# Output product of the token mixers in split one-pass products

## Chip, cores and metric

One core of a Trainium2 chip runs the whole program. The metric is the device time in microseconds (us) of one execution. Three executions of the kernel before took 1275.85, 1275.85 and 1276.56 us, median 1275.85.

Engines: PE is TensorE, ACT is ScalarE, DVE is VectorE, POOL is GpSimd, SP issues most DMAs. PEld is the weight load of a product, which overlaps the product before it.

## What is computed

A decoder trunk of two layers on 256 tokens of width 1024. In each layer three token mixers (attention with a window, a selected and a compressed branch; a convolution; retention) read one input projection, and their concatenated output goes through `w_out`. A dense SwiGLU follows on layer 0, an expert SwiGLU (2 of 8) on layer 1.

```python
def token_mixer(h, w_in, ..., w_out):
    proj = h @ w_in
...
    o_a = nsa_mixer(q, k_c, v_c, k_s, v_s, k_w, v_w, gl, cmp_pe, cmp_w1, cmp_w2)
    o_b = conformer_conv(conv_in, conv_w, conv_b, conv_ln_g, conv_ln_b, conv_pw)
    o_c = retention(rq, rk, rv, rg, ret_gn)
    return jnp.concatenate([o_a, o_b, o_c], axis=-1) @ w_out

for l in range(DEPTH):
    h = rmsnorm(x, ln_attn[l])
    x = x + token_mixer(h, ...)
    h = rmsnorm(x, ln_ffn[l])
    x = x + (swiglu(h, ...) if l % 2 == 0 else moe_ffn(h, ...))
```

## The kernel before, in words

The five engines have instruction streams of their own, written by hand, and each executes its stream strictly in order. In a mixer all engines walk one list of stages, `MIXER[l]`: for each entry an engine issues what it has to do for that stage, or nothing. So one table (`HEAD`, `AHEAD`, `BESIDE`, `TAIL`) sets the order on PE, ACT and DVE at once, and moving an entry moves it on all of them. PSUM banks are handed out round robin along that list (`GROUP`); an engine says that a bank is full (`is_full`) or free (`is_free`), and others wait with `full` and `freed`.

The middle of a mixer is twelve attention units k = 0 to 11. In unit k, PE transposes the probabilities of unit k (`probT`, L664), runs the scores of unit k + 2 (`score`), the entries of `BESIDE[k]`, and then probability by value (`pv`). ACT copies the transposed probabilities from PSUM (L1308), exponentiates the scores of unit k + 2 (L1298), then does its share of `BESIDE[k]`. DVE takes the maximum of the scores (L1705, L1707), which the exponentials wait for, then does its share of `BESIDE[k]`, then scales the result of `pv` (L1712, L1716, L1719). `BESIDE` places the convolution, the retention, the compressed branch and the output product between the units.

The output product has four banks: `out` k is token tile i = k // 2 and column half h = k % 2. Its first stage `out` multiplies rows 4 to 7 of `catT` (convolution in 4, 5, written by ACT in `conv_pw`; retention in 6, 7, by ACT in `retcat`) by `w_out`, four full fp32 products of 512 columns. Its second stage, `out_rest`, adds rows 0 to 3 (attention, in `attn_sum`) in four more. An fp32 product is recorded as two matmuls. Then DVE adds the bank to `x` (L1833), PE transposes `x` (`xT`), and in layer 0 DVE and ACT split the result into a high and a low half (L1841, L1380, L1845).

Elsewhere the kernel already uses split products: a float32 operand becomes a high part in fp32r (a copy on ACT) and a low part (raw minus high, on DVE), and `three` adds high x high, high x low, low x high, each in one pass. `pre` makes the first feed-forward weights ready: per half two copies of 1024 words a partition on ACT (L1390) and one subtraction of 2048 on DVE (L1869).

```python
def three(o, ah, al, bh, bl, first, final):
    mm(o, ah, bh, first, False)
    mm(o, ah, bl, False, False)
    return mm(o, al, bh, False, final)
...
elif stage == "out":
    ...
        for c in range(KD // 2, KD):
            mm(o, catT[:, c, i * P:(i + 1) * P], w[:, c, :], c == KD // 2, False)
```

Of the kernel before, what the change touches and what calls it, by code (L numbers as in the profile page):

```python
# [7 lines left out]
F32 = mybir.dt.float32  # L8
# [7 lines left out]
P = 128  # L16
# [60 lines left out]
def conv(a, b):  # L77
# [76 lines left out]
VW, RET, CONV, QK, W1K, W1VN, WO = range(7)  # L154
LAST_READ = (None, ("rqk", 1, 0), ("kcv", 0, 0), ("ks", 0, 0), ("cmpkv", 0, 0), ("cmpkv", 0, 0),
# [105 lines left out]
def hybrid_trunk_kernel(nc, x_in, consts_in, params_in, mix_in, ffn_in, moe_in, router_in, final_in, out):  # L261
    with ExitStack() as ctx:
# [57 lines left out]
        ro = mix("ro", [P, NT, RET_HEADS, HD])  # L320
        gates = mix("gates", [P, NT, HEADS, 3])
# [22 lines left out]
        cacc = mix("cacc", [P, 2, NC, T])  # L344
# [54 lines left out]
        whM = [nc.alloc_sbuf_tensor_at(f"whM{h}", [P, KD, FC], F32R, offset=home_at[h]) for h in range(4)]  # L399
        beforeb = sb("beforeb", [P, P], BF16)  # L400
# [77 lines left out]
        s_rk = sem("s_rk")  # L478
        s_conv_in = [sem(f"s_conv_in{h}") for h in range(2)]
# [179 lines left out]
        def _(pe):  # L659
# [24 lines left out]
            def width_major(o, l, n, half):  # L684
# [5 lines left out]
                return last  # L690

# [49 lines left out]
            def mixer(l):  # L741
                for stage, k in MIXER[l]:
# [219 lines left out]
                    elif stage == "out":  # L962
# [1317 lines left out]
```

## Time and profile before

| | |
|---|---|
| median of 3 executions | 1275.85 us |
| the profiled execution | 1274.48 us |
| its span, first to last instruction | 1272.5 us |
| busy PE / PEld / DVE / ACT | 98% / 80% / 78% / 67% |
| TensorE clock granted, mean | 0.997 |
| chain that ended last | PE 92%, DVE 4%, ACT 2%, DMA 1%, issue 1% |
| layer 0 mixer / dense / layer 1 mixer / experts | to 158 / to about 350 / to 496 / to 1264 us |

The profiled execution lies 1.4 us under the median, and its span 2.0 us under its own time. A busy PE is not PE at its peak, since the ends of matmuls are modelled; what counts is the distance of starts.

### The profile page before, as it was taken

Reading aid. Unit: us, or ns where it says so; the run is one execution under the profiler, and the core shown is the slowest. Engines: PE = TensorE matmul, PEld = TensorE weight load, DVE = VectorE, ACT = ScalarE, POOL = GpSimd, SP = SyncE. Lnnn points to the kernel's source line nnn. Section 1 sums busy time; section 2 is a strip of 40 time slices with the busy share of each in tenths; the row PEclk is TensorE's granted clock in tenths of the full one; section 3 lists DMA queues with packets and bytes.
Section 4 is the critical chain, followed back from the end, with each engine's and each line's share of the span. In section 5 each row is a group of like instructions: output and inputs, shape, how many; then the busy total and the mean of one; then the engine's idle time right before and its main releaser. Section 6 shows DMA issues by size and latency. Waiting matters only on the chain.

```text
span 1272.5 us, 16272 instructions
## 1 busy us (share of the span) xinstructions
PE 1253.3 (98%) x6317; PEld 1015.6 (80%) x6317; DVE 996.7 (78%) x1110; ACT 857.3 (67%) x1225; POOL 31.4 (2%) x21
## 2 busy tenths in 40 slices
PE   9999999999999999999999999999999999999997
PEld 8797588888779866788888888888888888888885
DVE  4786465454569646998999989889889889889997
ACT  5435364444451544978878888878878878878885
POOL 0000000000000000010000000000000000000300
PEclk9999999999999999999999999999999999999998
DMA  9433194442521336899999999999999999999981
GB/s 366 169 143 133 67 387 174 175 190 103 198 100 71 143 132 271 335 404 373 391 371 371 389 380 375 388 369 377 396 369 379 389 374 357 396 373 353 416 368 39
DMA packets 38625, 367.62 MB, mean 289 GB/s; under 512 B 4112, under 2 KB 7312, under 8 KB 11152
## 3 DMA queue, kind: packets, MB, share of 16 engines
q1 hardware_dynamic: 35808, 356.56, 71.2%
q0 software_dynamic: 1440, 5.24, 1.1%
q10 hardware_dynamic: 1296, 4.72, 0.9%
q8 instruction: 53, 0.87, 0.3%
q14 instruction: 28, 0.23, 0.1%
HBM read 360.73 MB, written 5.77 MB: 288 GB/s over the span
## 4 chain that ended last, share of the span: by engine, by line
PE 92%; DVE 4%; ACT 2%; DMA 1%; issue 1%; SPq 0%; DVEq 0%; ACTq 0%
PE ps L661 88%; PE ps L664 3%; DMA ring<-mix_in 1%; ACT arena L1298 1%; DVE blocks L1687 1%; DVE wlU L1869 1%; DVE arena L1705 0%; DVE wlD L1876 0%; ACT arena L1308 0%; ACT L1290 0%; ACT L1345 0%; DVE arena L1778 0%; DVE xn L2112 0%; DVE hTl L1991 0%; DVE x L1833 0%
## 5 line engine op out<-in xcount | busy, mean ns | idle before, releaser
L1869 DVE TENSOR_TENSOR wlU<-ring,whU 128x2048 fp32r<-128x2048 f32 x196 | 448.9, 2290 | 57.7 <-ACT whU L1390 53.1
L1390 ACT ACTIVATE whU<-ring 128x1024 fp32r<-128x1024 f32 x396 | 417.6, 1060 | 60.8 <-PE ps L661 53.2
L661 PE MATMUL ps<-whU,hTh 128*128 128x512 f32 x880 | 352.7, 401 | 0.8 <-DVE wlU L1869 0.8
L661 PE MATMUL ps<-whU,hTl 128*128 128x512 f32 x880 | 345.0, 392 | 0.0
L661 PE MATMUL ps<-wlU,hTh 128*128 128x512 f32 x880 | 342.9, 390 | 0.0
L1876 DVE TENSOR_TENSOR wlD<-ring,whD 128x2048 fp32r<-128x2048 f32 x97 | 222.2, 2290 | 39.2 <-ACT whD L1402 39.0
L1402 ACT ACTIVATE whD<-ring 128x1024 fp32r<-128x1024 f32 x194 | 205.2, 1066 | 59.0 <-PE ps L661 52.8
L661 PEld LDWEIGHTS ps<-whU,hTl 128*128 128x128 f32 x880 | 165.1, 188 | 36.0
L661 PEld LDWEIGHTS ps<-wlU,hTh 128*128 128x128 f32 x880 | 166.1, 189 | 32.4
L661 PEld LDWEIGHTS ps<-whU,hTh 128*128 128x128 f32 x880 | 165.3, 188 | 32.7 <-DVE wlU L1869 1.0
L661 PE MATMUL ps<-whD,gTh 128*128 128x512 f32 x428 | 168.6, 394 | 0.5 <-DVE gTl L1894 0.5
L661 PE MATMUL ps<-whD,gTl 128*128 128x512 f32 x428 | 167.3, 391 | 0.0
L661 PE MATMUL ps<-wlD,gTh 128*128 128x512 f32 x428 | 166.6, 389 | 0.0
L661 PEld LDWEIGHTS ps<-whD,gTh 128*128 128x128 f32 x428 | 80.4, 188 | 19.7 <-DVE wlD L1876 3.6
L661 PEld LDWEIGHTS ps<-whD,gTl 128*128 128x128 f32 x428 | 80.3, 188 | 16.9
L661 PEld LDWEIGHTS ps<-wlD,gTh 128*128 128x128 f32 x428 | 80.7, 189 | 16.4
L1416 ACT ACTIVATE gTh<-ps 128x256 fp32r<-128x256 f32 x107 | 40.3, 386 | 54.6 <-PE ps L664 54.6
L661 PEld LDWEIGHTS ps<-arena 128*128 128x128 f32 (+1 forms) x472 | 56.6, 190 | 14.5 <-issue 12.7
L661 PE MATMUL ps<-arena 128*128 128x64 f32 (+6 forms) x472 | 65.2, 297 | 2.3 <-ACT arena L1308 2.3
L1894 DVE TENSOR_TENSOR gTl<-ps,gTh 128x256 fp32r<-128x256 f32 x107 | 44.3, 422 | 27.5 <-ACT gTh L1416 27.5
L664 PE MATMUL ps<-cst,arena 128*128 128x128 f32 x376 | 63.3, 273 | 1.2 <-DVE arena L1815 1.1
L664 PEld LDWEIGHTS ps<-cst,arena 128*128 128x128 f32 x376 | 48.2, 143 | 17.2 <-issue 3.6
(232 smaller groups left out, 1224.2 us busy)
## 6 DMA issues: line engine op xcount, KB each, us to landing
ring<-moe_in SPq DMA_DIRECT2D x88, 2048.0 KB, 8.5
ring<-moe_in SPq DMA_DIRECT2D x88, 1024.0 KB, 8.6
ring<-ffn_in SPq DMA_DIRECT2D x11, 2048.0 KB, 7.5
ring<-mix_in SPq DMA_DIRECT2D x5, 3072.0 KB, 11.0
ring<-ffn_in SPq DMA_DIRECT2D x11, 1024.0 KB, 7.2
ring<-mix_in SPq DMA_DIRECT2D x4, 2048.0 KB, 10.3
ring<-mix_in SPq DMA_DIRECT2D x2, 2176.0 KB, 8.3
ring<-mix_in SPq DMA_DIRECT2D x2, 2112.0 KB, 8.1
```

What stands on the lines that cost most here:

```text
L661: return nc.tensor.matmul(o, lhsT, rhs, start=first, stop=last, skip_group_check=True)
L664: return nc.tensor.transpose(o, a, ident)
L1298: last = A(prob[:, k % 3, c * keys:(c + 1) * keys], bank(l, stage, k)[:, c * keys:(c + 1) * keys], ACT.Exp, bias=nmax[:, k, c:c + 1], scal ...
L1390: A(whU[:, p, :], ring[:, f.slot(J), p * PIECE:(p + 1) * PIECE], ACT.Copy).then_inc(s_hi, 1)
L1402: A(wh_down(f, J, c), ring[:, f.slot(J), (UP + c) * PIECE:(UP + c + 1) * PIECE], ACT.Copy)\
L1416: A(g_high(f, J, i), ps[:, up_bank(f, J, i), 0:FC].rearrange("p (c t) -> p c t", c=DOWN), ACT.Copy)\
L1687: last = V.tensor_tensor(blocks[lo:lo + HD, v, hi, :, g, 0:NBLK], src[g * HD:(g + 1) * HD, v, :, hi:hi + NBLK, r], spread(pe_[lo:lo + HD, ...
L1869: V.tensor_tensor(wlU[:, w, :], raw, whU[:, w, :].bitcast(F32), ALU.subtract).then_inc(s_lo, 1)
L1876: V.tensor_tensor(wl_down(f, J), raw, high.bitcast(F32), ALU.subtract).then_inc(s_lo, 1)
L1894: V.tensor_tensor(g_low(f, J, i), ps[:, up_bank(f, J, i), 0:FC].rearrange("p (c t) -> p c t", c=DOWN), g_high(f, J, i).bitcast(F32), ALU.s ...
```

## The change

`out` and `out_rest` are made of split one-pass products. For that, each layer gets:

- a stage `wo` k, k = 0 to 7: a quarter of one column half of `w_out` (two rows c of 512, 1024 words a partition). ACT copies it to `woh` (high), DVE writes raw minus high back over the raw words in the ring. `BESIDE[5]` to `BESIDE[11]` get one each, `TAIL` the last. PE waits for `s_wol` before each pair of rows.
- the concatenation in two parts: ACT writes `cath` (where `catT` was), DVE now also reads the bank and writes `catl`, and it is DVE that frees the bank. This holds for `conv_pw`, `retcat` and `attn_sum`.
- another order: `retcat` moves from unit 8 to unit 9, `out` 0 from unit 8 to 9, `out` 1 from 9 to 11, `out` 3 from 11 to `TAIL`; both `pre` stages come later in `TAIL`.

```diff
-AHEAD = {6: [("convB", 0), ("hidT", 0), ("hidT", 1), ("rsilu", 0), ("rroot", 0)], 8: [("retcat", 0)]}
+AHEAD = {6: [("convB", 0), ("hidT", 0), ("hidT", 1), ("rsilu", 0), ("rroot", 0)], 9: [("retcat", 0)]}
...
-          3: [("reto", 0), ("hid", 0), ("cnorm", 0)], 4: [("croot", 0), ("hid", 1), ("retnorm", 0)], 5: [("cnorm", 1)],
-          6: [("retnorm", 1)], 7: [("cmpkv", 0), ("conv_pw", 0)],
-          8: [("cscore", 0), ("out", 0)], 9: [("out", 1)],
-          10: [("cprobT", 0), ("out", 2), ("cpv", 0), ("cpv", 1)],
-          11: [("out", 3), ("asum", 0), ("asum", 1), ("osum", 0), ("attn_sum", 0)]}
-
-TAIL = [("osum", 1), ("pre", 0), ("out_rest", 0), ("attn_sum", 1), ("pre", 1), ("out_rest", 1), ("out_rest", 2), ("xT", 0),
-        ("xT", 1), ("out_rest", 3), ("xT", 2), ("xT", 3)]
+          3: [("reto", 0), ("hid", 0), ("cnorm", 0)], 4: [("croot", 0), ("hid", 1), ("retnorm", 0)],
+          5: [("cnorm", 1), ("wo", 0)], 6: [("retnorm", 1), ("wo", 1)], 7: [("cmpkv", 0), ("conv_pw", 0), ("wo", 2)],
+          8: [("cscore", 0), ("wo", 3)], 9: [("out", 0), ("wo", 4)],
+          10: [("cprobT", 0), ("out", 2), ("wo", 5), ("cpv", 0), ("cpv", 1)],
+          11: [("out", 1), ("wo", 6), ("asum", 0), ("asum", 1), ("osum", 0), ("attn_sum", 0)]}
+
+TAIL = [("osum", 1), ("wo", 7), ("out", 3), ("out_rest", 0), ("attn_sum", 1), ("pre", 0), ("out_rest", 1), ("out_rest", 2),
+        ("pre", 1), ("xT", 0), ("xT", 1), ("out_rest", 3), ("xT", 2), ("xT", 3)]
...
+WO_ROWS = ((0, 4), (0, 6), (0, 0), (0, 2), (1, 4), (1, 6), (1, 0), (1, 2))
...
+            def out_row(l, o, i, h, c, first, final):
+
+                if c % 2 == 0:
+                    pe.wait_ge(s_wol, len(WO_ROWS) * l + WO_ROWS.index((h, c)) + 1)
+                t = slice(i * P, (i + 1) * P)
+                low = ringl[:, mix_load(l, WO + h) % SLOTS, 512 * c:512 * (c + 1)]
+                return three(o, cath[:, c, t], catl[c // 2][:, c % 2, t], woh[l][2 * h + (c < 4)][:, c % 4, :], low, first, final)
...
+                    elif stage == "wo":
+                        h, c = WO_ROWS[k]
+                        n = mix_load(l, WO + h)
+                        act.wait_ge(slot_full[n % SLOTS], filled(n))
...
+                        A(wo_high(l, k), wo_rows(ring, l, k), ACT.Copy).then_inc(s_woh, 1)
...
+                    elif stage == "wo":
+                        dve.wait_ge(s_woh, len(WO_ROWS) * l + k + 1)
+                        V.tensor_tensor(wo_rows(ringl, l, k), wo_rows(ring, l, k), wo_high(l, k).bitcast(F32), ALU.subtract)\
+                            .then_inc(s_wol, 1)
+                    elif stage in ("conv_pw", "retcat"):
+                        m = 4 if stage == "conv_pw" else 6
+                        dve.wait_ge(s_cath, CATS * l + (m == 6) + 1)
+                        is_free(V.tensor_tensor(catl[m // 2][:], bank(l, stage).rearrange("p (q t) -> p q t", q=2),
+                                                cath[:, m:m + 2, :].bitcast(F32), ALU.subtract), l, stage)
```

DVE in layer 0 from the end of the compressed branch's softmax in unit 8 to the maximum of unit 11's scores. Before:

```order
L1761 TENSOR_REDUCE arena<-arena 128x16 [waits s_cexp]
L1762 RECIPROCAL arena<-arena 128x16 [waits v_done]
L1763 TENSOR_TENSOR arena<-arena 128x16 [waits v_done]
L1765 TENSOR_TENSOR arena<-arena,cst 128x128 x2
L1768 TENSOR_TENSOR arena<-arena 128x256 [waits v_done]
L1712 RECIPROCAL arena<-arena 128x2 [waits s_exp]
L1716 TENSOR_TENSOR arena<-arena 128x2 [waits v_done]
L1719 TENSOR_TENSOR arena<-ps,arena 128x128 [waits bank_full0,v_done]
L1705 TENSOR_REDUCE arena<-ps 128x2 [waits bank_full2]
L1707 TENSOR_SCALAR arena<-arena 128x2 [waits v_done]
```

With the change (line numbers are those of the changed kernel):

```order
L1798 TENSOR_REDUCE arena<-arena 128x16 [waits s_cexp]
L1799 RECIPROCAL arena<-arena 128x16 [waits v_done]
L1800 TENSOR_TENSOR arena<-arena 128x16 [waits v_done]
L1802 TENSOR_TENSOR arena<-arena,cst 128x128 x2
L1805 TENSOR_TENSOR arena<-arena 128x256 [waits v_done]
L1856 TENSOR_TENSOR ringl<-ring,woh_75 128x1024 [waits s_woh]
L1749 RECIPROCAL arena<-arena 128x2 [waits s_exp]
L1753 TENSOR_TENSOR arena<-arena 128x2 [waits v_done]
L1756 TENSOR_TENSOR arena<-ps,arena 128x128 [waits bank_full7,v_done]
L1861 TENSOR_TENSOR catl_86<-ps,cath 128x512 [waits s_cath]
L1742 TENSOR_REDUCE arena<-ps 128x2 [waits bank_full2]
L1744 TENSOR_SCALAR arena<-arena 128x2 [waits v_done]
```

The piece `wo` 3 and the low half of `retcat`, whose end frees `out` 0, now stand behind the softmax and ahead of the next maximum.

ACT in layer 0 from the exponentials of unit 8 to those of unit 10's scores. Before:

```order
L1298 ACTIVATE arena<-ps,arena 128x256 [waits bank_full5,s_amax]
L1298 ACTIVATE arena<-ps,arena 128x256
L1308 ACTIVATE arena<-ps 128x512 [waits s_exp,bank_full6,bank_full4]
L1298 ACTIVATE arena<-ps,arena 128x128 [waits bank_full0,s_amax]
L1298 ACTIVATE arena<-ps,arena 128x128 x3
L1355 ACTIVATE arena<-ps 128x512 [waits s_exp,bank_full1]
L1308 ACTIVATE arena<-ps 128x512 [waits bank_full3,bank_full7]
L1355 ACTIVATE arena<-ps 128x512 [waits bank_full4]
L1298 ACTIVATE arena<-ps,arena 128x256 [waits bank_full6,s_amax]
```

With the change:

```order
L1325 ACTIVATE arena<-ps,arena 128x256 [waits bank_full5,s_amax]
L1325 ACTIVATE arena<-ps,arena 128x256
L1392 ACTIVATE woh_74<-ring 128x1024 [waits s_exp,slot_full0]
L1335 ACTIVATE arena<-ps 128x512 [waits bank_full6,bank_full4]
L1325 ACTIVATE arena<-ps,arena 128x128 [waits bank_full0,s_amax]
L1325 ACTIVATE arena<-ps,arena 128x128 x3
L1382 ACTIVATE cath<-ps 128x512 [waits s_exp,bank_full1]
L1392 ACTIVATE woh_75<-ring 128x1024 [waits slot_full0]
L1335 ACTIVATE arena<-ps 128x512 [waits bank_full3,bank_full7]
L1325 ACTIVATE arena<-ps,arena 128x256 [waits bank_full6,s_amax]
```

Each copy of probabilities (L1308, now L1335) stands behind a copy of weights, and `retcat`'s copy has left.

DVE in layer 0 at the end of the mixer, from the first sum into `x`. Before:

```order
L1833 TENSOR_TENSOR x<-ps,x 128x512 [waits bank_full4]
L1869 TENSOR_TENSOR wlU<-ring,whU 128x2048 [waits s_hi]
L1833 TENSOR_TENSOR x<-ps,x 128x512 [waits bank_full5]
L1833 TENSOR_TENSOR x<-ps,x 128x512 [waits bank_full6]
L1841 TENSOR_TENSOR hT<-ps,par 128x4x128 [waits bank_full2]
```

With the change:

```order
L1886 TENSOR_TENSOR x<-ps,x 128x512 [waits bank_full4]
L1867 TENSOR_TENSOR catl_83<-ps,cath 128x2x128 [waits s_cath]
L1867 TENSOR_TENSOR catl_84<-ps,cath 128x2x128
L1922 TENSOR_TENSOR wlU<-ring,whU 128x2048 [waits s_hi]
L1886 TENSOR_TENSOR x<-ps,x 128x512 [waits bank_full5]
L1886 TENSOR_TENSOR x<-ps,x 128x512 [waits bank_full6]
L1922 TENSOR_TENSOR wlU<-ring,whU 128x2048 [waits s_hi]
L1894 TENSOR_TENSOR hT<-ps,par 128x4x128 [waits bank_full2]
```

The second subtraction of `pre` now stands between the third sum into `x` and the first use of the transposed `x`.

## Rows read from the trace of the kernel before

**Rows 1.** Page, part 4, the chain that ended last: shares of the span
```profile
PE 92%; DVE 4%; ACT 2%; DMA 1%; issue 1%; SPq 0%; DVEq 0%; ACTq 0%
```

**Rows 2.** Chain in order of time, layer 0: start us, us, what
```profile
107.42 0.60 ACT arena L1308
...
114.10 0.61 ACT arena L1308
...
114.84 1.08 PE ps L661 x8
...
136.92 3.44 PE ps L661 x8
...
145.61 6.88 PE ps L661 x16
```

**Rows 3.** Timeline of PE in the dense stage: start, duration; eleven starts apart
```profile
200.03 0.39 PE L661 MATMUL ps<-whD,gTl 128*128 128x512 f32 x1
...
202.53 0.39 PE L661 MATMUL ps<-wlD,gTh 128*128 128x512 f32 x1
```

**Rows 4.** Groups by line, whole program: busy us, mean ns | idle before
```profile
L1390 ACT ACTIVATE whU<-ring 128x1024 fp32r<-128x1024 f32 x396 | 417.6, 1060 | 60.8 <-PE ps L661 53.2 <-ACT ystage L1494 3.2
L1862 DVE TENSOR_TENSOR wlU<-ring,whU 128x1024 fp32r<-128x1024 f32 x4 | 4.8, 1224 | 4.5 <-ACT whU L1390 4.5
L1894 DVE TENSOR_TENSOR gTl<-ps,gTh 128x256 fp32r<-128x256 f32 x107 | 44.3, 422 | 27.5 <-ACT gTh L1416 27.5
L1841 DVE TENSOR_TENSOR hT<-ps,par 128x512 f32<-128x512 f32 x4 | 2.7, 682 | 0.0
L1196 ACT ACTIVATE xn<-x 128x512 f32<-128x512 f32 x20 | 12.5, 624 | 17.2 <-DVE x L1833 8.2 <-DVE x L1914 4.0 <-DMA x<-x_in 3.4
```

**Rows 5.** Timeline of ACT and DVE in layer 0, units 6 to 8
```profile
115.85 0.17 DVE L1707 TENSOR_SCALAR arena<-arena 128x4 f32<-128x4 f32 x1
116.05 0.37 ACT L1298 ACTIVATE arena<-ps,arena 128x128 f32<-128x128 f32 x1 [1.35 <-DVE arena L1707]
117.68 0.60 ACT L1355 ACTIVATE arena<-ps 128x512 f32<-128x512 f32 x1
118.54 0.17 DVE L1707 TENSOR_SCALAR arena<-arena 128x2 f32<-128x2 f32 x1
119.70 0.62 DVE L1750 SCALAR_TENSOR_TENSOR arena<-ps,cst 128x64 f32<-128x64 f32 x4 [0.99 <-PE ps L661]
123.06 0.42 DVE L1768 TENSOR_TENSOR arena<-arena 128x256 f32<-128x256 f32 x1
```

**Rows 6.** Chain in order of time, end of layer 0's mixer and layer 1's: start us, us, what
```profile
152.52 0.69 DVE x L1833
...
157.19 0.61 DVE x L1833
...
491.66 0.70 DVE x L1833
```

**Rows 7.** Busy time by stretch: PE, PEld, DVE, ACT, POOL, clock, DMA
```profile
119.60:131.00 11.40, 11.40 (x51) 7.17 (x50) 5.43 (x22) 3.23 (x12) 0.00 (x0) 1.00 0.41 172
131.00:144.00 13.00, 13.00 (x49) 7.18 (x48) 4.14 (x9) 4.52 (x7) 0.00 (x0) 1.00 0.00 1
```

**Rows 8.** The same at the program's end, after PE's last product
```profile
1264.00:1265.00 1.00, 0.00 (x0) 0.00 (x0) 1.00 (x4) 0.79 (x3) 0.00 (x0) 1.00 0.00 0
1265.00:1266.00 1.00, 0.00 (x0) 0.00 (x0) 0.96 (x2) 0.89 (x3) 0.00 (x0) 0.86 0.06 16
1266.00:1267.00 1.00, 0.00 (x0) 0.00 (x0) 1.00 (x3) 0.83 (x4) 0.00 (x0) 0.50 0.00 0
```

**Rows 9.** Timeline of PE: last product; filler products at the start and in layer 1
```profile
1263.51 0.39 PE L661 MATMUL ps<-yel,gTh 128*128 128x512 f32 x1
...
1.12 5.91 PE L661 MATMUL ps<-warm 128*128 128x256 bf16 x30 [1.12 <-POOL warm L2146]
...
496.45 1.69 PE L661 MATMUL ps<-warm 128*128 128x256 bf16 x14
```

More of the change, by code:

```diff
@@ L399, in hybrid_trunk_kernel @@
         whM = [nc.alloc_sbuf_tensor_at(f"whM{h}", [P, KD, FC], F32R, offset=home_at[h]) for h in range(4)]
+        wo_at = (xn_at, hT_at, ring_at + 4 * 4096, arena_at + 4 * mix_at["rp0"])
+        woh = [[nc.alloc_sbuf_tensor_at(f"woh{l}{q}", [P, 4, 512], F32R,
+                                        offset=wo_at[q] + 4 * SLOT * (mix_load(l, WO + 1) % SLOTS) * (q == 2))
+                for q in range(4)] for l in range(DEPTH)]
+        cath = nc.alloc_sbuf_tensor_at("cath", [P, KD, T], F32R, offset=arena_at + 4 * mix_at["catT"])
+        catl = [nc.alloc_sbuf_tensor_at(f"catl{q}", [P, 2, T], F32R,
+                                        offset=arena_at + 4 * (mix_at["cln"], mix_at["csq"], mix_at["cacc"], mix_at["cacc"] + 512)[q])
+                for q in range(4)]
         beforeb = sb("beforeb", [P, P], BF16)
@@ L478, in hybrid_trunk_kernel @@
         s_rk = sem("s_rk")
+        s_woh = sem("s_woh")
+        s_wol = sem("s_wol")
+        s_cath = sem("s_cath")
         s_conv_in = [sem(f"s_conv_in{h}") for h in range(2)]
@@ L540, in piece_of, with wo_rows, wo_high @@
             return w[:, :, col:col + FC]
+        def wo_rows(buf, l, q):
+            h, c = WO_ROWS[q]
+            return buf[:, mix_load(l, WO + h) % SLOTS, 512 * c:512 * (c + 2)].rearrange("p (c n) -> p c n", c=2)
+        def wo_high(l, q):
+            h, c = WO_ROWS[q]
+            return woh[l][2 * h + (c < 4)][:, c % 4:c % 4 + 2, :]
         def half_of(i, h):
@@ L1349, in mixer @@
                         full(act, l, stage, k)
-                        is_free(A(catT[:, 0:4, k * P:(k + 1) * P],
-                                  bank(l, stage, k).rearrange("p (q t) -> p q t", q=4), ACT.Copy), l, stage, k)
+                        A(cath[:, 0:4, k * P:(k + 1) * P], bank(l, stage, k).rearrange("p (q t) -> p q t", q=4), ACT.Copy)\
+                            .then_inc(s_cath, 1)
                     elif stage in ("conv_pw", "retcat"):
@@ L1354, in mixer @@
                         m = 4 if stage == "conv_pw" else 6
-                        is_free(A(catT[:, m:m + 2, :], bank(l, stage).rearrange("p (q t) -> p q t", q=2), ACT.Copy),
-                                l, stage)
+                        A(cath[:, m:m + 2, :], bank(l, stage).rearrange("p (q t) -> p q t", q=2), ACT.Copy)\
+                            .then_inc(s_cath, 1)
+                    elif stage == "wo":
+                        h, c = WO_ROWS[k]
+                        n = mix_load(l, WO + h)
+                        act.wait_ge(slot_full[n % SLOTS], filled(n))
+                        if k == 0:
+                            full(act, l, "kcv")
+                        elif k == 6:
+                            full(act, l, "retcat")
+                        A(wo_high(l, k), wo_rows(ring, l, k), ACT.Copy).then_inc(s_woh, 1)
                     elif stage == "pre":
@@ L1374, in mixer @@
                             act.wait_ge(s_root, NT * 3 + i + 1)
+                            full(act, l, "out", 2)
                             A(xh[:, i, :], x[:, i, :], ACT.Copy, scale=stat[:, 3, i:i + 1]).then_inc(s_xh, 1)
@@ L1816, in mixer @@
                             .then_inc(s_cln, 1)
+                    elif stage == "wo":
[7 more added lines that the diff above has]
+                                                cath[:, m:m + 2, :].bitcast(F32), ALU.subtract), l, stage)
+                    elif stage == "attn_sum":
+                        dve.wait_ge(s_cath, CATS * l + 2 + k + 1)
+                        t = slice(k * P, (k + 1) * P)
+                        for q in range(2):
+                            last = V.tensor_tensor(catl[q][:, :, t], bank(l, stage, k).rearrange("p (q t) -> p q t", q=4)
+                                                   [:, 2 * q:2 * q + 2, :], cath[:, 2 * q:2 * q + 2, t].bitcast(F32), ALU.subtract)
+                        is_free(last, l, stage, k)
                     elif stage == "asum":
```

15 lines of the change are left out of this document (6 added, 9 removed).

## Prediction

> **What bounds the kernel now.** I read the page's chain first [rows 1]: PE carries 92% of the span, so whatever leaves PE's path can shorten it, and whatever makes PE wait lengthens it. Then the chain in order of time through the middle of layer 0's mixer [rows 2]. It runs over ACT from the exponentials of unit 7 to the copy that starts at 114.10, and from 114.84 it stays on PE until the third sum into x at 152.52 [rows 6]. So the mixer has two halves: up to unit 7 the handshakes of ACT and DVE set the pace, from there PE does. In the second half PE is busy without a gap, while DVE is idle for half of the time and ACT for more than that [rows 7]. Layer 1 repeats layer 0 some 334.8 us later (the same rows, the same gaps; only the tail differs).
>
> **What it removes.** Four fp32 products of 512 columns take 3.44 us [rows 2], as the 6.88 for two stages confirms. In the dense stage eleven starts of one-pass products span 2.50 us [rows 3], 0.227 each, so twelve take 2.73. I take that for the new products, whose operands have the same shape. A stage saves 0.71 us, and eight stages in two layers save 16 x 0.71 = **11.4 us** of PE work.
>
> **What it adds.** Per layer on ACT eight copies of 1024 words at 1.06, on DVE eight subtractions of the same size at 1.22, two of 512 words at about 0.68 and four of 256 words at 0.42 [rows 4]. That is 8.5 us on ACT and 12.8 us on DVE. By busy time there is room for it. But these engines run in order, and each piece is put between two links of the loop that feeds PE: maximum (DVE), exponentials (ACT), piece (ACT), piece (DVE), scaling of pv (DVE), next maximum (DVE). I walk that loop through layer 0 in the times of the trace, with its durations and start distances. No DMA is added, and the second half of `w_out` is requested when the compressed branch's product is full, long before `wo` 4; SP's next loads wait for the end of `out_rest` as before, and need not be early.
>
> - Units 5 and 6: `wo` 0 and `wo` 1 stand on ACT ahead of the copies that start at 107.42 and 114.10 [rows 2], where ACT is the chain. Each costs 0.95 (the next starts while one drains). pv 7 on PE starts at 116.7 instead of 114.84: **+1.9**.
> - Unit 6 on DVE: `wo` 1's subtraction waits for ACT (116.1) and ends at 117.4; with the scaling behind it (0.74) and the maximum the exponentials of unit 9 start at 118.95 instead of 116.05 [rows 5].
> - Unit 7: ACT needs 1.6 for those exponentials, then `conv_pw`'s copy at 120.6 (117.68 before), then `wo` 2 to 122.1, then the copy of probabilities 8 to 122.6. PE, at cscore 2.0 late, is idle some 1.6 us until pv 8 at 122.75; before, `out` 0 filled that place. DVE takes `conv_pw`'s low half to 121.9, `wo` 2 to 123.4, the scaling to 124.0, and has the maximum of unit 10 ready at 124.8. Before, that was 118.7 [rows 5].
> - Unit 8: the softmax of the compressed branch starts at 124.75 instead of 119.70 and ends after 3.8 us (119.70 to 123.48 [rows 5]) at 128.5. Then `wo` 3 to 129.6, the scaling of pv 8 to 130.2, and only then the low half of `retcat`, to 130.8. That one frees `out` 0.
> - PE: pv 8, the transposes and the scores of unit 11 are done by 125.4. Then it waits for `retcat` until 131.0: **5.6 us idle**, the largest term.
> - From there PE has 12.7 us of work up to the end of `out` 1 (three stages at 2.73 and what the trace has between them), to 143.7. The attention sum needs both `asum` and `osum`, which stand behind `wo` 6 on DVE, which waits for ACT's copy behind the last copy of probabilities. They end at 146.2: **2.5 us idle**.
> - The rest of PE's work is 12.7 us to the end of `out_rest` 2 at 159.0. DVE ends the third sum at 160.1, but then `pre` 1's subtraction (2.2) stands ahead of the first use of the transposes. The chain of the tail, 4.6 us between the two sums in layer 0 [rows 6], becomes 6.8. The fourth sum ends at 166.9 instead of 157.8: layer 0 is **9.1 us** longer.
> - Layer 1: the same up to `out_rest`. There ACT's share of `pre` 1 stands behind two squares at 0.62 [rows 4] and a root, about 2 us together, and DVE waits for it. The fourth sum ends 11.2 us later than it does now (at 491.66 [rows 6]): **+11.2**.
>
> The sum is 9.1 + 11.2 = 20.3 us, after the 11.4 that PE saves. Nothing behind the mixers gets less work: dense and expert stages are PE without a gap and take the shift as it is.
>
> **The clock.** The trace of before has no PE idle of 5 us inside the program. Its nearest row is the end: the last product starts at 1263.51 [rows 9], the granted clock is still full until 1265, 0.86 in the next microsecond and 0.50 from 1266 [rows 8]. So it falls within some 2 us of idling, and a gap of 5.6 us before `out` 0 should see it fall. What that costs: at the kernel's start 30 filler products took 5.91 us, 0.197 each, in layer 1 fourteen took 1.69, 0.12 each [rows 9]. For 30 that is a loss of 2.3 to 2.7 us, the second with the last one's latency left out. The ends are 0 (the clock holds) and 2.7; I take 2.7 per layer since the end of the program is the nearest row: **+5.4 us**. The Trainium skill ("TensorE: Matmul & The Clock Gate", "Why this matters for your kernels") says that an idle gap between bursts of matmuls brings the half clock back. By that rule 2.7 per layer stands, without it the time would be that of the second rival. The end of this trace agrees with it (0.50 after the last product).
>
> Sum against the profiled execution: 1274.48 + 20.3 + 5.4 = 1300.2. That execution lies 1.4 us under the median, so the forecast is **1301.6 us** for the median, 2.0% more.
>
> **Rivals.**
> - *The clock falls at the tails too.* PE is idle for 3 to 5 us there, broken only by transposes. Two more times 2.7: 1307.
> - *The clock holds.* For it speaks that it was never below 1.00 in the mixers, though PE does little there. 1275.85 + 20.3 = 1296.
> - *The waits are half as long.* My walk adds handshakes one after another; if ACT and DVE absorb half of the net loss, +10: 1286.
> - *PE's saving wins, faster.* The place is the stretch from 114.84 on. Where DVE and ACT are idle for half of the time [rows 7], all pieces could fit into those gaps, and then 11.4 us come off: 1264.5. It decides if `retcat`'s low half is ready when PE reaches `out` 0, that is at 125.4 and not at 130.8. Against it: DVE's gaps are waits for PE, and its stream is in order. The Trainium skill ("Perfetto Trace Analysis", "Identifying the Most-Contended Engine") would have the engine with the highest occupancy optimized first, which is PE here, and by that rule the time would be this one; the 92% of the chain [rows 1] agree, the ACT rows at 107.42 and 114.10 [rows 2] do not.
> - *The change doesn't do what it says.* If weight loads did not hide behind the new products, a product might cost what an fp32 record costs now, 0.43 (3.44 by eight [rows 2]), a stage 5.2 instead of 2.73. Half of the sixteen stages would show in full after the waits: 8 x 2.5 = +20, 1322. The dense stage has the same form without it [rows 3].
>
> **How the numbers follow.** Chances: forecast 0.37, clock holds 0.27, waits half as long 0.14, clock falls at the tails too 0.10, faster 0.06, no one-pass gain 0.04, and 0.02 for gains and losses that cancel. The range has to hold 8 in 10: from 1284, just under the halved waits, to 1309, just over the fourfold fall; only the last three cases lie outside. A measurement can tell about 0.2% (2.6 us) from no change. Slower: 0.37 + 0.27 + 0.14 + 0.10 + 0.04 = 0.92; same 0.02; faster 0.06.
>
> **What would show it.** In the changed profile: twelve products from first to last in 2.5 to 2.8 us; the copies of probabilities 6 and 7 each about 1 and 2 us later against the trace of before; PE idle for 5 to 6 us ahead of the first product of `out` 0, released by the DVE subtraction of `retcat`; 2 to 3 us idle ahead of `attn_sum` 0, released by `osum`; the second subtraction of `pre` between the third sum and hT. The start of dense at about 167.5 instead of 158.3. Under full clock those gaps alone give +20; a clock row under 1.00 right after the first gap decides between forecast and second rival. If the gap ahead of `out` 0 is under 2 us, the walk over units 6 to 8 is wrong and the time is nearer 1280 or below. If a product there takes 0.4 and not 0.23, the price of the products is.

## The result, and the profile after

| | before | after |
|---|---|---|
| median of 4 executions each | 1275.85 us | 1306.53 us |
| ratio | 1 | 1.0244 (1.0231 to 1.0256) |
| span of the profiled execution | 1272.5 us | 1305.2 us |
| TensorE clock granted, mean | 0.997 | 0.98 |
| dense stage starts | 158.3 us | 171.65 us |
| first product of the experts | 504.81 us | 537.01 us |

The kernel became 30.7 us slower; 1301.6 was forecast. The trace of after starts 0.77 us earlier than that of before (the exponentials of unit 7 at 105.45 against 106.22), so 0.77 is added below wherever its times are compared with forecast ones. Layer 0's mixer took 172.4 - 158.3 = 14.1 us more, layer 1's 32.2 - 13.35 = 18.9 more. These are 33.0 and not 30.7, since the profiled execution of before lies 1.4 us under its median and that of after 0.7 over.

The chain's shares by engine on the page, to be read against [rows 1], where PE had 92%:

```profile
PE 90%; DVE 5%; ACT 3%; issue 2%; DVEq 0%; POOL 0%; ACTq 0%; POOLq 0%
```

PE lost two points to DVE, ACT and "issue", though it had less to compute. What it waited for is shown by the view of waits (who waited, for whom, us in total, times, the longest). Of before:

```profile
PE ps L661 <- ACT arena L1308: 2.3, 6, 0.5
```

Of after:

```profile
PE ps L684 <- ACT arena L1335: 6.3, 7, 2.0
PE ps L684 <- issue: 6.3, 2, 3.7
PE ps L687 <- DVE arena L1878: 4.7, 2, 2.3
PE ps L687 <- DVE x L1886: 4.1, 3, 3.4
PE ps L687 <- DVE hTr L1894: 3.3, 1, 3.3
```

The first is the copy of probabilities, behind a piece. The second is the gap ahead of `out` 0, which the profile puts down to nobody: it ends with `retcat`'s low half. The third is `osum`, the last two are sums and turned rows of the tail, behind the late `pre`. In the timeline of layer 0 (start, duration, engine, what; in brackets the idle time before it and who ended it) each is one line:

```profile
107.60 0.58 ACT L1335 ACTIVATE arena<-ps 128x512 f32<-128x512 f32 x1
115.17 0.58 ACT L1335 ACTIVATE arena<-ps 128x512 f32<-128x512 f32 x1
115.90 1.54 PE L684 MATMUL ps<-arena 128*128 128x64 f32 x8 [1.99 <-ACT arena L1335]
118.11 0.37 ACT L1325 ACTIVATE arena<-ps,arena 128x128 f32<-128x128 f32 x1 [2.36 <-DVE arena L1744]
123.75 0.17 DVE L1744 TENSOR_SCALAR arena<-arena 128x2 f32<-128x2 f32 x1
129.27 0.68 DVE L1861 TENSOR_TENSOR catl<-ps,cath 128x512 fp32r<-128x512 f32 x1
130.05 0.77 PE L684 MATMUL ps<-woh,cath 128*128 128x512 f32 x1 [3.73 <-issue]
130.62 0.63 PE L684 MATMUL ps<-ringl,cath 128*128 128x512 f32 x1
131.05 0.63 PE L684 MATMUL ps<-woh,catl 128*128 128x512 f32 x1
...
135.86 0.48 PE L684 MATMUL ps<-woh,cath 128*128 128x512 f32 x1
...
138.51 0.40 PE L684 MATMUL ps<-woh,catl 128*128 128x512 f32 x1
138.74 2.71 PE L684 MATMUL ps<-arena 128*128 128x512 f32 x12
...
147.00 1.04 PE L687 MATMUL ps<-cst,arena 128*128 128x128 f32 x4 [2.33 <-DVE arena L1878]
147.83 1.81 PE L684 MATMUL ps<-arena 128*128 128x64 f32 x8
148.71 0.76 DVE L1867 TENSOR_TENSOR catl<-ps,cath 128x256 fp32r<-128x256 f32 x2 [1.85 <-ACT cath L1377]
149.40 0.77 PE L684 MATMUL ps<-woh,cath 128*128 128x512 f32 x1
...
154.31 0.40 PE L684 MATMUL ps<-woh,cath 128*128 128x512 f32 x1
...
170.93 1.07 PE L687 MATMUL ps<-cst,x 128*128 128x128 f32 x4 [3.42 <-DVE x L1886]
```

The twelve products of `out` 2 start between 135.86 and 138.51, 2.65 us for eleven distances, and the next stage starts at 138.74: 2.88 us for the stage, close to the 2.73 of the forecast. But the products of `out` 0 behind the gap start 0.43 apart instead of 0.24. Busy time by stretch, with the granted clock as the third number from the end, says why:

```profile
116.00:118.00 2.00, 2.00 (x12) 2.00 (x13) 1.90 (x7) 0.00 (x0) 0.00 (x0) 0.58 0.94 393
...
124.00:126.00 2.00, 2.00 (x7) 1.35 (x5) 1.45 (x7) 1.59 (x6) 0.00 (x0) 0.50 0.08 33
126.00:128.00 2.00, 0.32 (x1) 0.00 (x0) 1.90 (x7) 1.72 (x3) 0.00 (x0) 0.86 0.00 0
128.00:130.00 2.00, 0.00 (x0) 0.00 (x0) 1.93 (x6) 0.00 (x0) 0.00 (x0) 1.00 0.00 0
130.00:132.00 2.00, 1.95 (x5) 1.59 (x6) 0.72 (x2) 1.09 (x5) 0.00 (x0) 0.50 0.00 0
...
150.00:152.00 2.00, 2.00 (x6) 1.61 (x5) 1.87 (x3) 0.00 (x0) 0.00 (x0) 0.50 0.00 0
...
172.00:174.00 2.00, 2.00 (x6) 1.52 (x6) 1.29 (x2) 0.64 (x3) 0.00 (x0) 0.50 1.08 459
```

In layer 0 the clock is at its lower level (0.50, 1.2 GHz) not once but behind each of the waits: after the 2 us ahead of `pv` 7, again in unit 8, after the gap ahead of `out` 0, after the 2.3 us ahead of `attn_sum` 0, and after the 3.4 us ahead of the last transposes. In layer 1 it is 0.50 from 520 to 532 us, and the 32 router products there took 6.83 us; 3.64 before. But not every wait brings it down. Layer 1 has the same wait ahead of `pv` 7, and there the clock stays full behind it; it falls at 471 us, with two more waits (0.52 us ahead of 469.05, 1.03 ahead of 472.04):

```profile
466.04 1.08 PE L684 MATMUL ps<-arena 128*128 128x64 f32 x8 [1.98 <-ACT arena L1335]
...
466.00:468.00 2.00, 1.96 (x16) 1.93 (x17) 1.93 (x5) 0.00 (x0) 0.00 (x0) 1.00 1.03 442
468.00:470.00 2.00, 1.49 (x21) 1.11 (x19) 0.87 (x4) 1.63 (x9) 0.00 (x0) 1.00 0.98 418
```

So the clock falls at five places in layer 0 and at four in layer 1.

### The profile page after: what moved, and what is told of

It reads as the page before. It is cut to its first block, busy times and chain, and to the rows that moved or that the text cites. A ratio compares the mean times of both kernels' runs of the same rounds, so it can differ in the third digit from the quotient of the medians.

```text
span 1305.2 us, 16458 instructions
## 1 busy us (share of the span) xinstructions
PE 1265.8 (97%) x6381; PEld 1044.1 (80%) x6381; DVE 1021.0 (78%) x1138; ACT 872.5 (67%) x1241; POOL 28.8 (2%) x21
## 4 chain that ended last, share of the span: by engine, by line
PE 90%; DVE 5%; ACT 3%; issue 2%; DVEq 0%; POOL 0%; ACTq 0%; POOLq 0%
PE ps L684 86%; PE ps L687 4%; DVE wlU L1922 1%; ACT arena L1325 1%; DVE blocks L1724 1%; DVE arena L1742 0%; ACT whU L1427 0%; DVE wlD L1929 0%; ACT woh L1392 0%; ACT arena L1335 0%; DVE x L1886 0%; DVE arena L1874 0%; ACT xn L1223 0%; ACT L1317 0%; ACT L1372 0%
## 5 line engine op out<-in xcount | busy, mean ns | idle before, releaser
L684 PE MATMUL ps<-arena 128*128 128x64 f32 (+6 forms) x472 | 70.3, 311 | 6.8 <-ACT arena L1335 6.3
L684 PEld LDWEIGHTS ps<-arena 128*128 128x128 f32 (+1 forms) x472 | 60.4, 201 | 17.6 <-issue 14.6
```

The source lines that it names most:

```text
L684: return nc.tensor.matmul(o, lhsT, rhs, start=first, stop=last, skip_group_check=True)
```

## The experiments

Two claims were to be tested: that the waits come from pieces set in order into the loop over ACT and DVE, and that the clock takes the rest. Ratios are to runs of before on the same chip, whose median was 1274.9 to 1275.5 us.

### The order alone

Tables of the change without the `wo` stages, on the kernel before.

```diff
-AHEAD = {6: [...], 8: [("retcat", 0)]}
+AHEAD = {6: [...], 9: [("retcat", 0)]}
...
-          8: [("cscore", 0), ("out", 0)], 9: [("out", 1)],
+          8: [("cscore", 0)], 9: [("out", 0)],
...
-TAIL = [("osum", 1), ("pre", 0), ("out_rest", 0), ("attn_sum", 1), ("pre", 1), ("out_rest", 1), ("out_rest", 2), ("xT", 0),
-        ("xT", 1), ("out_rest", 3), ("xT", 2), ("xT", 3)]
+TAIL = [("osum", 1), ("out", 3), ("out_rest", 0), ("attn_sum", 1), ("pre", 0), ("out_rest", 1), ("out_rest", 2),
+        ("pre", 1), ("xT", 0), ("xT", 1), ("out_rest", 3), ("xT", 2), ("xT", 3)]
```

> Left out of the change: the split products, the eight pieces per layer and the low halves of the concatenation; only the new order of retcat, out and pre is kept, with fp32 products. Theory (the pieces and low halves, put between the links of the loop over ACT and DVE, make most of the waits): PE has the same work as before, out 0 no longer fills unit 8 (some 1 to 2 us per layer), and the second subtraction of pre stands in the tail (2.2 us in layer 0, some 4 in layer 1): 1276 + 9 = 1285 us (1280 to 1291), no clock row under 0.95 in the mixers but perhaps at the tails. Rival (the order itself is the cause: out no longer covers the units): the waits of the change are nearly all there, and without the 11.4 us that PE saves the time is 1305 or more.

Measured: 1284.8 us, ratio 1.0081 (1.0064 to 1.0097), +9.6 us. The rival falls. That the time is the expected one is in part luck: unit 8, which was to cost 1 to 2 us per layer, costs 0.4 in layer 0 (from the exponentials of unit 7 to the third sum 46.7 us against 46.3), and the clock, which the sum had at nothing, is 0.50 for some 14 us in layer 1's tail. The waits are those of the tail:

```profile
PE ps L664 <- DVE x L1833: 3.5, 2, 2.9
...
PE ps L664 <- DVE hTr L1841: 2.0, 1, 2.0
```

### The pieces alone

```diff
-          5: [("cnorm", 1)], 6: [("retnorm", 1)], 7: [("cmpkv", 0), ("conv_pw", 0)],
-          8: [("cscore", 0), ("out", 0)], 9: [("out", 1)],
+          5: [("cnorm", 1), ("wo", 0)], 6: [("retnorm", 1), ("wo", 1)], 7: [("cmpkv", 0), ("conv_pw", 0), ("wo", 2)],
+          8: [("cscore", 0), ("out", 0), ("wo", 3)], 9: [("out", 1), ("wo", 4)],
...
+                    elif stage == "wo":
...
+                        V.tensor_tensor(wo_high(l, k), wo_rows(ring, l, k), wo_high(l, k).bitcast(F32), ALU.subtract)\
+                            .then_inc(s_wol, 1)
```

> Kernel before with its order and its fp32 products, plus the eight pieces per layer (ACT's copy, DVE's subtraction) at the units where the change has them; their results are used by nothing. Theory: units 5 and 6 are ACT's path, so pv 7 comes 1.9 us later per layer; behind it out 0 and out 1 cover the pieces; in the tail the last piece costs up to 1 us: 1276 + 2 x 2.5 = 1281 us (1278 to 1288), clock full. Rival (ACT and DVE absorb the pieces): 1276 to 1277. Rival (the loop walks later by every piece, also under out 0 and out 1): 1276 + 2 x 8 = 1292 or more.

Measured: 1290.9 us, ratio 1.0127 (1.0110 to 1.0144), +15.7. My own number missed; the time lies by that of the last rival. Timeline of PE in layer 0 (this trace starts 0.46 us earlier than that of before):

```profile
116.21 1.08 PE L678 MATMUL ps<-arena 128*128 128x64 f32 x8 [1.98 <-ACT arena L1325]
...
120.07 1.96 PE L678 MATMUL ps<-arena 64*128 64x16 f32 x32 [0.92 <-ACTq L1320]
122.65 2.05 PE L678 MATMUL ps<-ring,arena 128*128 128x512 f32 x2 [0.62 <-ACT arena L1372]
...
146.63 0.63 PE L681 MATMUL ps<-cst,arena 128*128 128x128 f32 x4 [1.66 <-DVE arena L1855]
```

`pv` 7 is 1.8 us late as expected, but that isn't the end: the exponentials of unit 9 stand behind it, and `out` 0 starts at 122.65 where it started at 119.60, 3.5 us late with the offset. Up to there the clock is full, behind the wait of 1.98 us too; it is 0.61 and 0.54 in the rows from 122 to 126, and the piece `wo` 6 ahead of `asum` costs 1.7 more. `out` 0 hides nothing that was lost before it. In the prediction I had followed the loop through unit 7; in this expectation I stopped at `pv` 7.

### Holding the clock

```diff
+                        if k in (7, 8):
+                            keep_busy(o, 16 if k == 7 else 8)
...
+                            keep_busy(o, 42)
...
+                        if k == 0:
+                            keep_busy(o, 20)
...
+                        if k >= 2:
+                            keep_busy(ps[:, OUT_BANK[0], :], ((4, 28), (40, 6))[l][k - 2])
```

> The changed kernel plus bf16 filler products on PE in the gaps ahead of pv 7, pv 8, out 0, attn_sum 0 and the transposes of the third and fourth sums, sized by the trace to end before the wait does. Theory (the granted clock falls at four or five places of each mixer, not at one, and that costs about 10 us): 1306.5 - 10 = 1296.5 us (1294 to 1300), clock rows near 1.00 through both mixers. Rival (the low clock only falls where PE waits anyway): 1304 to 1308.

Measured: 1296.3 us, ratio 1.0168 (1.0151 to 1.0185), mean clock 0.995. That is 10.2 us less than the change (9.7 by the two ratios), for products that compute nothing. The rival falls. What is left, 21.1 us over before, is within 1 us of the 20.3 to which my walk of waits had come, and the layers agree one by one: 8.9 and 12.5 us more in this trace, 9.1 and 11.2 in the walk. One fall is left, in layer 1's tail (0.50 from 516 to 523 us), so 10.2 is the least that the clock took.

### `pre` back at its early places, alone and with the fillers

```diff
-TAIL = [..., ("out_rest", 0), ("attn_sum", 1), ("pre", 0), ("out_rest", 1), ("out_rest", 2), ("pre", 1), ("xT", 0), ...
+TAIL = [..., ("pre", 0), ("out_rest", 0), ("attn_sum", 1), ("pre", 1), ("out_rest", 1), ("out_rest", 2), ("xT", 0), ...
```

> The changed kernel with both pre stages back at their places in the order of before. Theory (the second subtraction of pre, 2.2 us, stands on the path of the tail; in layer 1 ACT's share of about 2 us too): 2.2 + 4.2 less, plus a clock that may hold at the tail: 1306.5 - 6.4 = 1300 us (1297 to 1303). Rival (the earlier pre pushes the low halves of the attention sum and the first sum into x later by as much): 1305 to 1309.

Measured: 1294.4 us, ratio 1.0151 (1.0134 to 1.0168): 12.1 us less than the change, more than either theory gave.

> The changed kernel with both edits that were tried alone: fillers ahead of pv 7, pv 8, out 0 and attn_sum 0 (not in the tail), and both pre stages back at their early places. Alone they gave 10.2 us (fillers, the tail's among them) and 12.1 us (pre). Theory (pre's own wait is 6.4 us and the rest of its 12.1 is the clock that no longer falls at the tail, so the two share the tail's part of the clock): 1306.5 - 10.2 - 6.4 = 1290 us (1288 to 1292). Rival (separate causes that add up in full): 1284. Rival (both are the clock alone): 1294 to 1296.

Measured: 1289.0 us, ratio 1.0110 (1.0095 to 1.0125), where the theory said 1290. So the two edits overlap. With the clock held, the early `pre` gives 1296.3 - 1289.0 = 7.3 us: that is its wait (my walk had 2.2 + about 4; the two traces show 2.2 in layer 0 and 4.4 in layer 1). Without it, 12.1: the other 4.8 are clock that the late `pre` took in the tails. In the traces the clock is low in the tails for some 17 us with the change and some 3 us with the early `pre`, and in units 6 to 11 for about as long in both. And with the early `pre` the fillers give 1294.4 - 1289.0 = 5.4: the clock behind the waits ahead of `pv` 7, `out` 0 and `attn_sum` 0. Each of these differences is uncertain by some 2 us, since the ratios' intervals reach 0.0015 to 0.0017 to either side.

### Which half of a piece, and POOL as the place for them

In the kernel with the subtractions on POOL, ACT keeps the copies:

```diff
-                    elif stage == "wo":
-                        dve.wait_ge(s_woh, len(WO_ROWS) * l + k + 1)
-                        V.tensor_tensor(wo_rows(ringl, l, k), ...
+                for k in range(len(WO_ROWS)):
+                    pool.wait_ge(s_woh, len(WO_ROWS) * l + k + 1)
+                    G.tensor_tensor(wo_rows(ringl, l, k), ...
```

> The changed kernel, but only the eight subtractions per layer go to POOL; ACT keeps the eight copies. It tells which half of a piece costs. Theory (both halves stand in the loop; ACT's cost about 2 us per layer up to unit 7 and again at its copies of probabilities later, DVE's the rest, above all ahead of the maximum of unit 10 and the low half of retcat): 1306.5 less about 12 = 1294 us (1288 to 1300). Rival (ACT's copies alone make it): 1303 to 1308. Rival (DVE's subtractions alone): near what the kernel with all pieces on POOL takes.

Measured: 1298.7 us, ratio 1.0188 (1.0171 to 1.0205), 7.8 less than the change. The counterpart has the copies on POOL (`G.tensor_copy`) and the subtractions on DVE:

> The counterpart of the kernel with the subtractions on POOL: the changed kernel with the eight copies per layer on POOL (early, as soon as the half of w_out is there) and the eight subtractions left on DVE. Theory (ACT's copies are half of the handshake, and a copy on POOL holds DVE up for at most its own 1.04 us, where the subtraction of 2.4 us held it for as long): DVE does not wait for ACT's copy any more, units 5 and 6 lose nothing: 1306.5 - 9 = 1297 us (1292 to 1301). Rival (DVE's subtractions alone bind units 7 and 8): 1303 to 1308. Rival (POOL's copies stretch DVE's short operations on the path of units 4 and 5): 1305 or more, with DVE operations of two operands in SBUF over 1 us long.

Measured: 1297.5 us, ratio 1.0172 (1.0155 to 1.0189), 9.0 less. Neither half makes the loss by itself; each is a link of the loop. How much each takes stays open, since POOL holds DVE up in both (below). Then both halves on POOL, in the order of the change and in that of before:

> The changed kernel and its order, but all eight pieces per layer (copy and subtraction) on POOL, which is idle there. ACT and DVE keep only the high and low parts of the concatenation. Theory (the waits come from pieces put in order into the loop over ACT and DVE): what is left is what the order alone costs (1284.8 - 1275.2 = 9.6 us, measured) plus some 1.5 us per layer for the low halves, less PE's 11.4: 1275.2 + 9.6 + 3 - 11.4 = 1276 us (1272 to 1284), clock rows near 1.00 but at the tails. Rival (POOL holds DVE up, or is so slow that PE waits for the pieces): 1290 or more. Rival (the low halves and the PE waits on them are what costs, not the pieces): 1300 or more.

> As the kernel with all pieces on POOL, but in the order of before (retcat and out 0 in unit 8, out 1 in 9, out 3 in 11, pre early in the tail). Theory: nothing is left of the change's cost but the low halves, of which retcat's (0.68 us) and the first attention sum's (0.84 us) are on PE's path: 1275.2 - 11.4 + 2 x 2.5 = 1269 us (1265 to 1277), faster than both kernels. Rival (with shorter products, PE runs ahead of the loop over ACT and DVE in units 8 to 11 and waits there for what it saved): 1275 to 1280. Rival (POOL's pieces, in particular the last of the second half, come too late for PE): 1285 or more.

Measured: 1306.1 us, ratio 1.0236 (1.0219 to 1.0253), and 1291.3 us, ratio 1.0127 (1.0105 to 1.0149). Both theories missed by far, and the times are those of the rivals. The reason is in DVE's groups (mean ns behind the comma). Of before:

```profile
L1716 DVE TENSOR_TENSOR arena<-arena 128x4 f32<-128x4 f32 x8 | 1.3, 164 | 0.3
L1787 DVE TENSOR_TENSOR arena<-arena 128x512 f32<-128x512 f32 x2 | 1.4, 692 | 0.1
```

The same instructions with both halves on POOL, in the order of the change:

```profile
L1744 DVE TENSOR_TENSOR arena<-arena 128x4 f32<-128x4 f32 x8 | 7.3, 910 | 0.3
L1815 DVE TENSOR_TENSOR arena<-arena 128x512 f32<-128x512 f32 x2 | 2.8, 1406 | 0.1
```

The time of 1306.1 also fits the rival that blamed the low halves of the concatenation. Against it speaks that `retcat`'s low half keeps its 0.68 us there; it starts at 135.96, behind a chain of such stretched instructions, and so PE waits 6.7 us ahead of `out` 0.

In the order of before, POOL and DVE side by side in the timeline of layer 0:

```profile
134.16 2.41 POOL L2208 TENSOR_TENSOR ringl<-ring,woh 128x1024 fp32r<-128x1024 f32 x1
134.47 2.12 DVE L1744 TENSOR_TENSOR arena<-arena 128x2 f32<-128x2 f32 x1
...
136.62 0.50 PE L684 MATMUL ps<-woh,cath 128*128 128x512 f32 x1 [1.88 <-POOL ringl L2208]
```

A DVE product of two numbers per partition, with both operands in SBUF, takes 0.16 us; here it ends with POOL's subtraction, after 2.12. The Trainium skill ("SBUF — State Buffer", "Who interferes with whom") says that a DVE instruction with two SBUF inputs contends with a GpSimd instruction that reads SBUF, and that the port pair which the two share is an exclusive lock. The two lines agree. With the copies alone on POOL the same group of eight has a mean of 0.34 us: held up too, but by shorter instructions. And in the order of before the second half of `w_out` only lands at 129.5, as unit 8 ends (its `pv` starts at 130.2), so that with both halves on POOL the last pieces, 3.5 us each, come late for PE (5.1 us of waits).

### A version that pays: split less, and where the engines are idle

The order of before; only `out_rest` is split. That takes four pieces a layer, and all stand in units 9 and 10. `conv_pw`, `retcat` and `out` stay fp32, and in `out_rest` the four products that need the low part of the concatenation come last.

```diff
-WO_ROWS = ((0, 4), (0, 6), (0, 0), (0, 2), (1, 4), (1, 6), (1, 0), (1, 2))
+WO_ROWS = ((0, 0), (0, 2), (1, 0), (1, 2))
...
+          8: [("cscore", 0), ("out", 0)], 9: [("out", 1), ("wo", 0)],
+          10: [("cprobT", 0), ("wo", 1), ("wo", 2), ("out", 2), ("wo", 3), ("cpv", 0), ("cpv", 1)],
...
+                        pe.wait_ge(s_cath, CATS * l + i + 1)
+                        for c in range(KD // 2):
...
+                            mm(o, cath[:, c, t], woh[l][2 * h + 1][:, c, :], False, False)
+                            mm(o, cath[:, c, t], ringl[:, mix_load(l, WO + h) % SLOTS, 512 * c:512 * (c + 1)], False, False)
+                        freed(pe, l, "attn_sum", i)
+                        for c in range(KD // 2):
+                            last = mm(o, catl[c // 2][:, c % 2, t], woh[l][2 * h + 1][:, c, :], False, c == KD // 2 - 1)
```

> A version meant to beat both: the order of before; only out_rest (rows 0 to 3) is split, with four pieces per layer instead of eight, put into units 9 and 10, where the trace of before has ACT and DVE idle and PE sets the pace; conv_pw, retcat and out stay as before; in out_rest the products with the low part of the concatenation come last, so that DVE's low half is covered. Theory (the change loses by where its pieces stand, not by what they are): PE saves 8 stages x 0.71 = 5.7 us, and the tail gives back up to 1: 1275.3 - 5.2 = 1270 us (1268.5 to 1273), clock full in the mixers. Rival (pieces cost about as much as they save wherever they stand): 1274.5 to 1277. Rival (DVE becomes the bound of the tail, with two subtractions of pre, four sums and the low halves): 1278 or more.

Measured: 1272.9 us, ratio 0.9980 (0.9971 to 0.9989): faster than both kernels, by 2.6 us against before and not by 5.2. From the exponentials of unit 7 to the dense stage layer 0 takes 2.0 us less than before (in the chain 105.76 to 156.13 here, 106.22 to 158.56 before). All of it is there at the third sum into x: the first three stages of `out_rest` take 2.0 us less, 0.66 each. The fourth saves nothing, because from the third to the fourth sum the chain runs over DVE and ACT, 4.67 us in both kernels; PE only waits 1.4 us there where it waited 0.7. In layer 1 the gain is gone at the router, and the layer takes 1.0 us more than before. So the two traces show 1.0 us of the 2.6; where the others come from stays open. Layer 1's tail:

```profile
484.99 0.63 PE L687 MATMUL ps<-cst,x 128*128 128x128 f32 x4 [1.44 <-DVE x L1889]
...
489.34 0.63 PE L687 MATMUL ps<-cst,x 128*128 128x128 f32 x4 [0.51 <-DVE x L1889]
489.81 5.06 PE L684 MATMUL ps<-router,hTr 128*128 128x8 f32 x32
```

DVE's subtraction of `pre` 1 ends just before the second sum, PE waits 1.4 us and 0.5 us, the clock is 0.50 from 492 to 498, and the router products take 5.06 us where they took 3.64. Two ways to mend that were tried. First, 11 and 4 fillers ahead of the second and the fourth transposes of layer 1:

```diff
+                        if l and k in (1, 3):
+                            keep_busy(ps[:, OUT_BANK[0], :], 11 if k == 1 else 4)
```

> The late version (only out_rest split, order of before; measured 0.998 of before) plus 11 and 4 filler products of 256 columns on PE in layer 1's tail, ahead of the transposes that wait 1.4 and 0.6 us for the second and fourth sum. In its trace the clock is 0.50 from 492 to 498 there and the 32 router products take 5.06 us instead of 3.64. Theory (two short waits bring the clock down, and that gives back part of the 5.7 us): the products are at 3.6 again, 1.5 us less: 0.998 becomes 0.9968 (0.9960 to 0.9975). Rival (the low clock is hidden there by DVE and ACT): 0.998 as it was. Rival (the fillers come late and delay the transposes): 0.9985 or more.

Measured: 1272.4 us, ratio 0.9978 (0.9969 to 0.9987). The products are at their old length:

```profile
491.18 3.64 PE L684 MATMUL ps<-router,hTr 128*128 128x8 f32 x32
```

Yet the time is hardly less: 0.9978 and 0.9980 can't be told apart, and the 0.9968 expected lies just outside the interval. By the number the rival holds, that the low clock is hidden; by the traces it doesn't. The chains of the two traces, from the exponentials of unit 7 in layer 0 to the end of the router in layer 1, show the gain and what covers it. Without the fillers:

```profile
105.76 1.03 ACT arena L1334 x4
...
499.40 9.72 PE ps L684 x56
```

With them:

```profile
107.16 1.03 ACT arena L1336 x4
...
499.04 9.72 PE ps L684 x56
```

That is 393.6 us without, 391.9 with them, and 394.6 before: the fillers win 1.8 us, as expected. But the same instruction of layer 0, which no edit touches, stands 1.4 us later in this execution. The start of the program varies by as much as is to be measured: over ten of the traces this instruction starts between 105.4 and 107.2. Second, `pre` 1 of layer 1 behind the last transposes:

```diff
-                           BESIDE[k] + [("pv", k)]] + TAIL for l in range(DEPTH)]
+                           BESIDE[k] + [("pv", k)]] + LAST[l] for l in range(DEPTH)]
...
+LAST = [TAIL, [z for z in TAIL if z != ("pre", 1)] + [("pre", 1)]]
```

> The same late version, but in layer 1 the second stage of pre stands behind the last transpose instead of between the second and the third attention half. In its trace DVE's subtraction of pre (481.95 to 484.15) ends just before the second sum, for which PE waits 1.4 us. Theory (DVE's order makes that wait, and the wait the low clock): 1.4 us of wait and 1.4 us of clock go, 0.998 becomes 0.9958 (0.9950 to 0.9970). Rival (pre is needed by SP for the next weights or by the experts, and comes too late now): 0.9985 or more. Rival (the path there runs over ACT's squares and not over pre): 0.998 as it was.

Measured: 1274.0 us, ratio 0.9992 (0.9983 to 1.0001). A miss. The second sum isn't waited for any more, but now `pre` 1 stands ahead of the router's work on DVE:

```profile
PE ps L685 <- DVE selb L2002: 2.4, 1, 2.4
```

and the clock is 0.50 from 494 to 502 instead. The wait was moved and had not gone.

## Why the prediction was right, and where it was off

- **The price of the products**: nearly right. 2.65 us for eleven distances in `out` 2, against 2.50 in [rows 3]; 0.09 of the difference is the first distance, behind transposes, the rest that the others are 0.233 and not 0.227. A stage takes 2.88 there against 3.44 before, so it saves 0.56, and 0.66 in the version that pays, where the sum had 0.71. Over sixteen stages the 11.4 us are too much by 1 to 2.
- **The walk over units 5 to 8**: right. Predicted and measured (with 0.77 added): `pv` 7 at 116.7 and 116.67; exponentials of unit 9 at 118.95 and 118.88; maximum of unit 10 ready at 124.8 and 124.7; `retcat`'s low half done at 130.8 and 130.7; `out` 0 at 131.0 and 130.8. The idle time ahead of it was 3.7 and not 5.6 us, because PE came to it later (scores of unit 11 at the low clock), not because the gap ended sooner. The predicted 1.6 us ahead of `pv` 8 are not idle in layer 0, where PE was late by the low clock, and show in layer 1, where it was full (0.52 + 1.03).
- **The sum of the waits less PE's saving**: right, and not by luck alone. 20.3 against 21.1 us with the clock held by fillers, 9.1 and 11.2 for the layers against 8.9 and 12.5. The 1 to 2 us of saving that did not come are within that.
- **The clock**: the term that was mis-sized. The step was "a gap of 5.6 us before `out` 0 should see it fall", one fall per layer at 2.7 us, 5.4 in all. The clock was low at five places in layer 0 and four in layer 1, and took 10.2 us or somewhat more. 5.4 of that belong to the waits in units 5 to 11 and 4.8 to the tails. That 5.4 is the forecast's number is luck: it is seven falls there, not two. The rival with falls at the tails (1307) was nearest to the time. Its argument, gaps of 3 to 5 us, was also too narrow: it fell behind a wait of 2.0 us in layer 0 as well, though not behind the same one in layer 1.
- **The low halves of the attention sum**: in the walk I had them in DVE's busy time and not on the path, and there they are. They run from 148.71 to 149.47; the products from 149.40 on are those of `out` 3, which don't need them, and `out_rest` 0 starts at 154.31.
- **The tail**: the part for `pre` was 2.2 + about 4, and measured 7.3 with the clock held (2.2 + 4.4 in the traces). The fourth sum of layer 0 ended 4.7 us later than predicted: all of that is clock. 1.6 stood already at `attn_sum` 0, as much as `out` 0 lost at the low clock (4.4 us for a stage of 2.8). 1.1 are the transposes of `attn_sum` 0 and `pv` 11 (147.00 to 149.40, 2.4 us for 1.3), and 2.1 the products from 149.40 on that started 0.43 apart.
- **Faster, with all pieces in the gaps**: the mechanism exists, but not at the places that the change chose. It works in units 9 and 10, with half of the pieces.

What stays open is the exact gain of the last versions. Within one trace the fillers of layer 1's tail win 1.8 us; the medians, whose intervals are some 1.1 us wide to either side, don't show it. That all eight stages could be split with profit, if the pieces of rows 4 to 7 stood late, wasn't tried.

## What to carry to other kernels

Before moving work to an engine with idle time, follow the loop that feeds the bound engine in order, one link after another, up to the point from which the bound engine really has a backlog. Work put ahead of that point costs about its duration, on ACT and DVE both; behind it, it is free as long as no wait follows on it. Here that point was unit 9: the four pieces in units 9 and 10 cost nothing up to the third sum, but the one ahead of `asum` in unit 11 cost 1.7 us. Four pieces placed so, with the order of before, won 0.2%, where eight, half of them ahead of unit 9, lost 2.4% together with the new order.

When a change makes TensorE wait, price the wait and then the clock behind it, at every wait that is new: here the clock came to half as much as all waits net of the saving (10.2 beside 21.1 us), though not every single wait brought it down. A run with filler products in the gaps separates the two.

A mended order should be read again as a whole: what leaves one wait stands ahead of another.

## What the runs showed of the hardware that was not expected

- The clock can fall after short waits too. Behind 1.99 us of idle PE in layer 0 it was 0.58, but behind 1.98 us at the same place of layer 1, and in layer 0 of the kernel with the pieces alone, it stayed at 1.00 for at least 4 us more; behind two waits of 1.4 and 0.5 us, with transposes and a stage of products between them, 0.50 for some 6 us. In a gap itself the row can stand at 1.00 again (128 to 130 us, no product at all) and be at 0.50 as soon as products follow. So a gap's own row says nothing on what it will cost.
- 32 router products of 8 columns, during which the weight loads were busy throughout (0.19 us each at the full clock, 0.33 at the low one, overlapping), took 3.64 us at the full clock, 5.06 in the version of which the clock fell during them, and 6.83 at 0.50 throughout: the clock also counts where few columns move.
- POOL copies 1024 words a partition in 1.04 us, as fast as ACT (1.05), but subtracts them in 2.41 us, twice as long as DVE (1.22). While it does, a DVE instruction with two operands in SBUF that starts behind it stands still until it ends, even the smallest. A TENSOR_SCALAR with one operand there does too, for 2.00 us where it takes 0.17; reciprocals and reductions keep their 0.16 and 0.68 us. With both halves on POOL, in the order of the change (POOL's subtraction runs from 136.89 to 139.26):

```profile
136.56 0.68 DVE L1733 TENSOR_REDUCE arena<-ps 128x2 f32<-128x512 f32 x1
137.28 2.00 DVE L1735 TENSOR_SCALAR arena<-arena 128x2 f32<-128x2 f32 x1
139.19 0.16 DVE L1740 RECIPROCAL arena<-arena 128x4 f32<-128x4 f32 x1
```
